# Half of the token stage's weights and its first two tiles loaded one stage earlier, and the order of that stage's opening

## The reference, cut to what matters

```
m = silu(cond) @ w_mod + b_mod                 # shift1, scale1, ...
h = rmsnorm(x, norm1_g) * (1 + scale1) + shift1
q, k, v, g = split(h @ w_in[:, 1536:3584], 4)  # 512 columns each
q, k = rope_2d(q), rope_2d(k * HD ** -0.5)
state = exp(log_sigmoid(decay) * 128) * state + (k * zeta).T @ v   # per tile of 128 tokens
```

## Time and profile before

| | |
|---|---|
| median of 3 runs | 3487.83 us (3487.07 to 3490.82) |
| the profiled execution's own time | 3487.38 us |
| its span | 3485.6 us |
| PE busy | 3204.7 us, 92% |
| DVE, ACT, POOL busy | 1608.5, 1276.7, 369.1 us |
| mean granted clock of PE | 0.954 of full speed |
| token stage | from 127 us to about 620 us of the span |

### The profile page before, as it was taken

How to read it: one execution, slowest core, us unless ns; L and a number is a source line. 1 busy time by engine, 2 the same in 40 slices (tenths; PEclk the granted TensorE clock), 3 DMA queues, 4 the chain that set the end, 5 groups by cost and what they waited for, 6 DMA issues and landing times. The chain is left out here.

```text
span 3485.6 us, 51370 instructions
## 1 busy us (share of the span) xinstructions
PE 3204.7 (92%) x19287; PEld 2742.7 (79%) x19287; DVE 1608.5 (46%) x2989; ACT 1276.7 (37%) x1947; POOL 369.1 (11%) x313
## 2 busy tenths in 40 slices
PE   7589999799979789999988982999999999999996
PEld 2278888798835779989987872988998898889895
DVE  5333223433345542332225557565555555556555
ACT  4544443322234031222114430444444444344445
POOL 1011111000033200000000001011111111112112
PEclk9899999999989789999999985999999999999998
DMA  9533332411199852341206442455555555555557
GB/s 337 193 119 107 105 123 86 147 56 62 56 324 346 284 174 84 99 128 60 93 31 213 151 141 81 162 196 202 197 194 187 178 183 172 171 172 200 195 205 277
DMA packets 281637, 565.66 MB, mean 162 GB/s; under 512 B 22296, under 2 KB 161432, under 8 KB 277289
## 3 DMA queue, kind: packets, MB, share of 16 engines
q1 hardware_dynamic: 257023, 503.83, 41.5%
q0 software_dynamic: 15456, 54.88, 5.3%
q10 hardware_dynamic: 8976, 4.46, 0.4%
HBM read 434.44 MB, written 128.64 MB: 162 GB/s over the span
## 5 line engine op out<-in xcount | busy, mean ns | idle before, releaser
L71 PE MATMUL experts_bank<-experts_xT_high,experts_w_high_gu 128*128 128x272 f32 x2048 | 598.6, 292 | 5.5 <-DVE experts_w_low_gu L2896 5.5
L73 PE MATMUL experts_bank<-experts_xT_high,experts_w_low_gu 128*128 128x272 f32 x2048 | 591.3, 289 | 0.0
L72 PE MATMUL experts_bank<-experts_xT_low,experts_w_high_gu 128*128 128x272 f32 x2048 | 589.9, 288 | 0.0
L71 PEld LDWEIGHTS experts_bank<-experts_xT_high,experts_w_high_gu 128*128 128x128 f32 x2048 | 386.2, 189 | 18.4 <-issue 12.2
L72 PEld LDWEIGHTS experts_bank<-experts_xT_low,experts_w_high_gu 128*128 128x128 f32 x2048 | 386.8, 189 | 4.0
L73 PEld LDWEIGHTS experts_bank<-experts_xT_high,experts_w_low_gu 128*128 128x128 f32 x2048 | 386.7, 189 | 0.0
L2896 DVE TENSOR_TENSOR experts_w_low_gu<-experts_w_raw_gu,experts_w_high_gu 128x1024 fp32r<-128x1024 f32 x256 | 302.2, 1215 | 12.5 <-ACT experts_w_high_gu L2695 12.4
L2695 ACT ACTIVATE experts_w_high_gu<-experts_w_raw_gu 128x1024 fp32r<-128x1024 f32 x256 | 257.4, 1047 | 19.7 <-DMA experts_w_raw_gu<-in_w_stream 19.6
L71 PE MATMUL merge_pg<-merge_hT_high,merge_w_gates_high 128*128 128x436 f32 (+1 forms) x640 | 231.9, 362 | 13.4 <-DVE merge_hT_low L2015 13.3
L72 PE MATMUL merge_pg<-merge_hT_low,merge_w_gates_high 128*128 128x436 f32 (+1 forms) x640 | 231.3, 361 | 0.0
L73 PE MATMUL merge_pg<-merge_hT_high,merge_w_gates_low 128*128 128x436 f32 (+1 forms) x640 | 230.9, 361 | 0.0
(11 more groups left out here) (385 smaller groups left out, 6627.5 us busy)
## 6 DMA issues: line engine op xcount, KB each, us to landing
experts_w_raw_gu<-in_w_stream SPq DMA_DIRECT2D x256, 512.0 KB
experts_w_raw_d<-in_w_stream SPq DMA_DIRECT2D x128, 512.0 KB, 6.3
filters_wm<-in_w_mod SPq DMA_DIRECT2D x12, 2048.0 KB, 12.8
merge_hT<-scratch_hT SPq DMA_DIRECT2D x32, 436.0 KB, 7.2
scratch_h<-out_row SPq DMA_DIRECT2D x17, 520.0 KB, 2.8
tokens_x<-in_xs SPq DMA_DIRECT2D x17, 512.0 KB, 5.3
scratch_hT<-tokens_hT SPq DMA_DIRECT2D x17, 512.0 KB, 4.4
scratch_qkT<-tokens_qkT SPq DMA_DIRECT2D x17, 512.0 KB, 2.8
```

The source lines that it names most:

```text
L71: pe.matmul(out, lhs[0], rhs[0], start=start, stop=False)
L72: pe.matmul(out, lhs[0], rhs[1], start=False, stop=False)
L73: return pe.matmul(out, lhs[1], rhs[0], start=False, stop=stop)
```

## The change

Eight of the 16 weight pieces are loaded in the filter stage. A new area `w_early` of eight pieces, with `x_early` and `rope_early` behind it, lies at the same addresses as `wm`: pieces 0 to 3 in its first slot, 4 to 7 in its second, x and the rotary tables of two tiles in the third. SP issues them when PE has used each slot for the last time: at p = 7 after chunk 9, at p = 9 after chunk 10, at p = 11 after chunk 11. Their semaphores live through all stages. In the token stage `qkT`, `vs`, `vz`, `gs`, `kvb`, `state`, `kvf` and `qk` are put at the start of memory, over `w_early`; x and rope are the early areas themselves. So the first state can be loaded only after all 16 pieces are split, and ACT's back(0) and DVE's turn(0) stand behind the splits.

The other eight pieces are loaded into the eight places of `w_early`, each after the piece that it replaces is split. ACT and DVE start with the front of tile 0 between the first splits, take the norm of tile 1 after eight of them, the rest of the splits, and only then the decays. The first two tiles' code is written out ahead of the loops. PE's own order is as it was.

```diff
+                    if p in (7, 9):
+                        sp.wait_ge(PM.sem, PM.at(9 if p == 7 else 10, "parts"))
+                        for m in range(4 * (p == 9), 4 + 4 * (p == 9)):
+                            n, k = PIECES[m]
+                            sp.dma_start(s["w_early"][:, m].rearrange("p (a b) -> p a b", b=512), d["w_qkvg"][n, :, k:k + 2, :])\
+                              .then_inc(s["ld_w_early"][m], 16)
+                    if p == 11:
+                        sp.wait_ge(PM.sem, PM.at(11, "parts"))
+                        for h in range(2):
+                            sp.dma_start(s["x_early"][:, h, :], d["xs"][take(h, 1)]).then_inc(s["ld_x_early"][h], 16)
+                            sp.dma_start(s["rope_early"][:, h, :], d["rope"][take(h, 1)]).then_inc(s["ld_rope_early"][h], 16)
...
+EARLY = 8
+TILE_WORDS = 17 * 512
+PIECES = [(n, k) for n in range(4) for k in range(0, KT, 2)]
...
+        "ld_w_early": [sem(f"ld_w_early{m}") for m in range(EARLY)],
+        "ld_x_early": [sem(f"ld_x_early{h}") for h in range(2)],
+        "ld_rope_early": [sem(f"ld_rope_early{h}") for h in range(2)],
     }
+
+    base = nc.sbuf_base
+    s["w_early"] = nc.alloc_sbuf_tensor_at("w_early", [P, EARLY, 1024], F32, offset=base)
+    s["x_early"] = nc.alloc_sbuf_tensor_at("x_early", [P, 2, DM], F32, offset=base + 4 * TILE_WORDS)
+    s["rope_early"] = nc.alloc_sbuf_tensor_at("rope_early", [P, 2, 512], F32, offset=base + 4 * (TILE_WORDS + 2 * DM))
+    return s
...
+        qkT = sb("qkT", [P, 2, 2, 512])
+        vs = sb("vs", [P, 2, 512])
+        vz = sb("vz", [P, 2, 512])
+        gs = sb("gs", [P, 2, 512])
+        kvb = sb("kvb", [P, 2, 512])
+        state = sb("state", [P, 2, 512])
+        kvf = sb("kvf", [P, 512])
+        qk = sb("qk", [P, 2, 512])
+        sb("early", [P, 2 * DM + 1024])
+        x = s["x_early"]
+        rope = s["rope_early"][:].rearrange("p a (b c) -> p a b c", b=4)
...
-                sp.dma_start(state[:, 0, :], d["state_f"]).then_inc(ldc, 16)
...
-                load_x(0, 0)
-                load_x(1, 1)
-                load_rope(0, 0)
-                load_rope(1, 1)
-                for m, (n, k) in enumerate(PIECES):
-                    if m >= 3:
-                        sp.wait_ge(w_dve, m - 2)
-                    sp.dma_start(staged[m % 3].rearrange("p (a b) -> p a b", b=512), d["w_qkvg"][n, :, k:k + 2, :])\
-                      .then_inc(ldw[m % 3], 16)
-                sp.wait_ge(ldc, 64)
+                for m in range(EARLY, len(PIECES)):
+                    n, k = PIECES[m]
+                    sp.wait_ge(w_dve, m - EARLY + 1)
+                    sp.dma_start(early[:, m % EARLY].rearrange("p (a b) -> p a b", b=512), d["w_qkvg"][n, :, k:k + 2, :])\
+                      .then_inc(ldw[m % EARLY], 16)
+                sp.wait_ge(w_dve, len(PIECES))
+                sp.dma_start(state[:, 0, :], d["state_f"]).then_inc(lds, 16)
+                sp.wait_ge(ldc, 48)
+                sp.wait_ge(lds, 16)
...
-                log_decays_scalar(act, tmp, ca, cv)
-                act.wait_ge(cv, 9)
-                for n in range(2):
-                    act.activation(zeta[:, 4 * n:4 * n + 4], lg[:, 4 * n:4 * n + 4], ACT.Exp, scale=expo[:, n:n + 1])\
-                       .then_inc(cs, 1)
-                act.activation(dec[:], lg[:], ACT.Exp, scale=float(P)).then_inc(cs, 1)
-                act.wait_ge(cs, 4)
-
-                def front(t, h, cond, k):
+                act.wait_ge(cs, 1)
+
+                def decays():
+                    log_decays_scalar(act, tmp, ca, cv)
+                    act.wait_ge(cv, 9)
+                    for n in range(2):
+                        act.activation(zeta[:, 4 * n:4 * n + 4], lg[:, 4 * n:4 * n + 4], ACT.Exp, scale=expo[:, n:n + 1])\
+                           .then_inc(cs, 1)
+                    act.activation(dec[:], lg[:], ACT.Exp, scale=float(P)).then_inc(cs, 1)
+
+                def split(m):
+                    n, k = PIECES[m]
+                    act.wait_ge(ldw[m % EARLY], 16 * (m // EARLY + 1))
+                    act.activation(wh[:, n, k:k + 2].rearrange("p a b -> p (a b)"), early[:, m % EARLY], ACT.Copy)\
+                       .then_inc(w_act, 1)
+
+                def norm(t, h, k):
...
-                front(0, 0, 0, 0)
-                for m, (n, k) in enumerate(PIECES):
-                    act.wait_ge(ldw[m % 3], 16 * (m // 3 + 1))
-                    act.activation(wh[:, n, k:k + 2].rearrange("p a b -> p (a b)"), staged[m % 3], ACT.Copy)\
-                       .then_inc(w_act, 1)
-                with act.Fori(0, LOOP // 2, 1) as i:
+                norm(0, 0, 0)
+                split(0)
+                scale(0, 0)
+                split(1)
+                split(2)
+                turned(0, 0, 0)
+                for m in range(3, EARLY):
+                    split(m)
+                norm(1, 1, 0)
+                scale(1, 1)
+                for m in range(EARLY, len(PIECES)):
+                    split(m)
+                decays()
+                turned(1, 1, 0)
+                act.wait_ge(w_dve, len(PIECES))
+                back_1(0, 0, 0)
+                front(2, 0, 0, 1)
+                back_1(1, 1, 0)
+                with act.Fori(1, LOOP // 2, 1) as i:
...
-                v.wait_ge(ldc, 64)
-                log_decays_vector(v, lg, raw, tmp, ca, cv)
-                v.wait_ge(cs, 4)
-
-                def front(t, h, cond, k):
+
+                def split(m):
+                    n, k = PIECES[m]
+                    v.wait_ge(w_act, m + 1)
+                    flat = lambda a: a[:, n, k:k + 2].rearrange("p a b -> p (a b)")
+                    v.tensor_tensor(flat(wl), early[:, m % EARLY], flat(wh).bitcast(F32), ALU.subtract).then_inc(w_dve, 1)
...
+                    if isinstance(t, int) and t == 0:
+                        v.wait_ge(lds, 16)
...
                 norm(0, 0)
-                front(0, 0, 0, 0)
-                for m, (n, k) in enumerate(PIECES):
-                    v.wait_ge(w_act, m + 1)
-                    flat = lambda a: a[:, n, k:k + 2].rearrange("p a b -> p (a b)")
-                    v.tensor_tensor(flat(wl), staged[m % 3], flat(wh).bitcast(F32), ALU.subtract).then_inc(w_dve, 1)
-                with v.Fori(0, LOOP // 2, 1) as i:
+                split(0)
+                split(1)
+                turned(0, 0, 0)
+                split(2)
+                low(0, 0)
+                for m in range(3, EARLY):
+                    split(m)
+                norm(1, 1)
+                for m in range(EARLY, len(PIECES)):
+                    split(m)
+                v.wait_ge(ldc, 48)
+                log_decays_vector(v, lg, raw, tmp, ca, cv)
+                v.wait_ge(cs, 4)
+                back_1(0, 0, 0)
+                front(1, 1, 0)
+                back_2(0, 0, 0)
+                norm(2, 0)
+                back_1(1, 1, 0)
+                front(2, 0, 0)
+                back_2(1, 1, 0)
+                with v.Fori(1, LOOP // 2, 1) as i:
...
```

More of the change, by code:

```diff
@@ L865, in front @@
                                    ACT.Copy).then_inc(*AF.inc("high"))
+                def front(t, h, cond, k):
+                    norm(t, h, k)
+                    scale(t, h)
+                    turned(t, h, cond)
                 def back_1(t, h, k):
@@ L918, in front @@
                      .then_inc(*VF.inc("low"))
+                def front(t, h, cond):
+                    turned(t, h, cond)
+                    low(t, h)
                 def norm(t, h):
@@ L972, in _ @@
                         back_1(i * 2 + h, h, i)
[L973 removed]
+                        front(i * 2 + (h + 1), 1 - h, 0)
                         back_2(i * 2 + h, h, i)
```

31 lines of the change are left out of this document (11 added, 20 removed).

## The result

The changed kernel takes 3453.41 us, the median of 4 runs (3451.82 to 3455.72), against 3488.66 us for four runs of the kernel before (3487.07 to 3490.82). The ratio is 0.9902, with a 95% interval of 0.989 to 0.9915. The forecast was 3456.5 us, in a range of 3451 to 3466. The profiled execution took 3455.72 us with a span of 3453.8, so between the two profiled executions (3487.38 before) the gain is 31.66 us, where 31.2 were worked out; between the two medians it is 35.25 us.

The account below looks back on a forecast made before the run. Weight loads through three landing places were taken to bound the token stage's opening; q(1) 32.3 us earlier, less 1.1 for the clock, gives 31.2 off 3487.4, rounded to 3456.5 us, range 3451 to 3466.

Parts of the forecast that it names:

- Filter stage, cost 0: Filter stage: 5.77 MB of added loads fit into free DMA slices and cost 0; 14.4 us if all lay open.
- Rival B: Filter stage: early loads delay the spectra's stores and hold ACT, giving 3462.5 us, or 3471 fully exposed; chance 8%.
- the prediction's own signs of a cost: Filter stage's end: `eps` memset outside 127 to 128 us, or ACT's waits for spectra stores beyond 5 us.
- To q(0): Token stage opening: ACT starts at about 127.5, and q(0) at 139.9 against 155.47, 15.5 us earlier.
- The splits: Weight splitting on DVE: after xn(1), eight subtractions at 1.235 us each, the last ending at 157.2.
- Decays, turn(0), hT(1), v: After the splits: decays 3.86 us, turn(0) 4.2, DVE's hT(1) done at 166.7, v copied out by 168.4.
- The added wait: hT of tile 1 waits for hT(0)'s store, queued on SP behind the state's load; costs 0 to 2.1 us.
- POOL: Before the kv products: first `vz` takes 1.02 us, so the first kv product starts at 169.5, the second at 170.6.
- The clock: PE rests from 166.5 to 169.5; if its clock falls q(1) loses 2.2 us, half charged, 1.1.
- The bound: Token stage opening: bound moves from loads to DVE's queue; PE's own row alone would put q(1) at 168.3.

Follow-up runs that it names:

- early store: Changed kernel with SP issuing the store of hT(0) between the loads of pieces 10 and 11, ahead of the state's load; 3454.14 us.
- the spare products: Changed kernel plus unread identity products on PE, 20 ahead of tile 0's transposes and 24 behind them; 3463.25 us, one run.
- the kernels with no wait of note in PE's row: Changed kernel with hT(0) stored early and DVE's hT(1) before turn(0), plus v copied first (3452.00 us) or decays moved to the filter stage (3451.88 us).

## Why the prediction was right, point by point

The path was right: the loads are no longer waited for, DVE's queue and the row behind it through ACT and POOL set q(1), and each step is within 2.3 us of its place. That the sum held to a tenth of a microsecond at q(1), 31.2 predicted and 31.21 measured, is luck: the splits, POOL, the clock and a later start of the whole stage were off, and cancelled. All times after `eps`:

| step | predicted | measured |
|---|---|---|
| q(0) starts | 12.65 | 12.02 |
| last subtraction ends | 29.95 | 27.84 |
| decays end | 33.85 | 31.63 |
| turn(0) ends | 38.05 | 35.95 |
| DVE's hT(1) ends | 39.45 | 37.24 |
| v copied | 41.15 | 38.87 |
| first kv product | 42.25 | 40.67 |
| q(1) | 44.15, 45.25 with the clock | 43.89 |

*Filter stage, cost 0: right, with a later start that is not its doing.* The eight pieces take 8.0 us each to land beside other traffic, and ACT's waits for the spectra's stores grow by 1.2 us:

```profile
w_early<-in_w_qkvg SPq DMA_DIRECT2D x8, 512.0 KB, 8.0
```
```profile
ACT filters_spec L448 <- DMA scratch_kspec<-filters_spec: 6.6, 2, 3.4
```
```profile
ACT filters_spec L437 <- DMA scratch_kspec<-filters_spec: 5.4, 2, 2.9
```

The second row is of the kernel after, the third of the kernel before. The bytes went into the free slices of the earlier trace rows:

```profile
GB/s 235 408 359 235 303 396 371 346 427 284 260 297 396 427 359 325 362 396 417 408 424 331 300 390 411 411 291 402 210 339 410 422 450 359 0 303 433 93 244 152
```

The mean between 75 and 128 us rose from 218 to 335 GB/s. Rival B's place for a cost was right, its price was not paid: from the first spectra's store to `eps` it is 67.28 us before and 67.30 after. The 1.33 us later start was there already at that first store (59.97 before, 61.28 after), before any early load is issued. In the ten experiments that store lies between 59.23 and 62.44 us and `eps` between 127.06 and 129.75, and the distance between the two is the same with early loads and without. Two of the prediction's own signs of a cost did show, `eps` at 128.58 in place of 127 to 128 and 6.6 us of waits for the stores in place of 5; by this distance neither was one.

*To q(0): right, 0.6 early.* ACT started 0.09 us after the memset (0.25 was taken). The copy of piece 0, behind ACT's table load, put 0.55 us between the square and `xn` (3.61 us in place of 3.06), where 0.76 was taken, so `xn` was 0.35 early at 3.70:

```profile
128.67 1.06 ACT L877 ACTIVATE tokens_xn<-x_early 128x1024 f32<-128x1024 f32 x1 [3.82 <-DVE tokens_eps L952]
129.64 0.19 ACT L877 ACTIVATION_READ_ACCUMULATOR tokens_xn<-x_early 128x1 f32 x1
129.84 1.28 ACT L880 ACT_TABLE_LOAD   x1
...
132.28 1.13 ACT L884 ACTIVATE tokens_xn<-x_early,tokens_rstd 128x1024 f32<-128x1024 f32 x1
```

The other 0.3 us came from DVE's steps, which followed each other more closely than I had taken.

*The splits: mis-sized by 2.1 us, to the good.* I took 1.235 us a subtraction, a little over the mean of 1.224 of ten, most of which followed a wait. In a row they take 1.15 (9.18 / 8, and 5.76 / 5 in the fronts), because the 1.22 us of one overlap its neighbour's by 0.07. Over the twelve subtractions from the fourth to the last that is 1.0 us; 0.6 was there at q(0), and 0.5 is hand-overs that I had put too high.

*Decays, turn(0), hT(1), v: right.* 3.88 us where 3.86 were taken, 4.29 for 4.2, 1.37 for 1.4, and `vs` within 0.2 us of its distance from hT(1).

*The added wait: right at 0.* The state's load took 2.5 us to land, the value taken; I had put the cost of the wait between 0 and 2.1 us. SP's rows after, and ACT's:

```profile
156.44 0.33 SPq L776 DMA_DIRECT2D tokens_state<-in_state_f  x1
159.49 0.70 SPq L746 DMA_DIRECT2D scratch_hT<-tokens_hT  x1
```
```profile
163.72 1.50 ACT L891 ACTIVATE tokens_hT<-tokens_tp,shift,scale 128x128 f32<-128x128 f32 x4 [3.51 <-issue]
165.90 1.06 ACT L897 ACTIVATE tokens_h_high<-tokens_hT 128x1024 fp32r<-128x1024 f32 x1 [0.68 <-ACT tokens_hT L891]
166.87 0.58 ACT L909 ACTIVATE tokens_vs<-tokens_pv 128x512 f32<-128x512 f32 x1
```

ACT did stand 3.51 us until the store had landed, 4.2 us after its issue (4.4 were taken), but `h_high(1)` needs DVE's half as well, and that ended at 165.82. The early store left the kv products where they were. The Trainium skill, in "DMA: Bandwidth & Descriptors", section "Anatomy of one DMA", has a fixed time plus a time for the bytes, which gave an estimate of 2.6 us for the state's load; that section is written for transfers that GpSimd issues, and this one is issued by SP. This trace's 2.5 is close to it all the same.

*POOL: mis-sized by 0.7 us.* Two `vz` took 2.04 us before and 2.49 now, and with the hand-overs the first kv product came 1.80 us after `vs` in place of 1.1.

```profile
167.62 2.49 POOL L1070 TENSOR_TENSOR tokens_vz<-tokens_vs,tokens_zeta 128x512 f32<-128x512 f32 x2 [60.09 <-ACT tokens_vs L909]
```

*The clock: near in size, wrong in place.* I charged 1.1 us to the projection q(1), half of 2.2, for a clock that might fall. It did fall, in the kv products: they took 3.22 us from the first to q(1), 1.3 more than at the upper clock, and q(1) itself lost about 0.2, for the clock was back at 1.00 from 173 us on. The rest that preceded it was 1.93 us and not 3. The Trainium skill, in "TensorE: Matmul & The Clock Gate", section "The HAM clock gate", has PE's clock fall after idleness, and says that the moment of a change is not tied to the kernel's own start and varies from run to run. The traces agree that the length of the rest alone does not settle it: at these same products the clock stayed at 1.00 after rests of 2.42 and 2.74 us and fell after 1.93 and 3.49.

So up to `vs` the stage ran 2.3 us ahead of my sum; POOL gave back 0.7 and the clock in the kv products 1.3, which leaves 0.3; the later start of the stage, which is not the change's doing, took 1.33, where 1.1 had been set aside for the clock. The 1.1 stood in the sum for another reason, so this agreement is luck. The median of the runs lies 2.3 us below the profiled execution, which the forecast could not know: the profiled one was the slowest of four.

*The bound.* The prediction said that the bound goes from the loads to DVE's queue, and that PE's own row would put q(1) at 168.3, which is 41.05 after `eps`. Both were shown: the spare products moved PE's row forward and q(1) followed DVE's, and the kernels with no wait of note in PE's row have q(1) at 40.30 and 40.77 (0.6 of the distance to 41.05 is the earlier q(0)).

*What the prediction did not see* is how the gain is shared. It followed one path and never asked which part of the change carries it. By the runs the loads in the filter stage are worth 6.9 us with the new order (8.2 at a like clock) and nothing with the old one, and the eight places are worth 21.8.

## What to carry to other kernels

When loads feed a split through few places and each place is refilled only after its piece is used, count places against landing time divided by the pace of the split: three places at 4.6 us per load held a 1.15 us step to 2.2 us, and eight removed nearly all of it without any earlier load. A prefetch gains where the work that needs it stands first in its engine's queue; here it was worth nothing behind 6 us of small loads and the decays. Reorder and prefetch together, and test each alone. A bound that is one wait ahead of the next, as here with POOL, ACT and PE within 4 us, gives little back for any single further edit.

## What the runs showed of the hardware

- PE's clock fell after a rest of 1.93 us in one execution and not after 2.42 us in another with the same products on both sides, nor after 2.74 us in a third, so the length of a rest alone did not decide it. In the spare-products kernel it fell after 3.49 us.
- When the clock fell, it did so after PE had begun again: the microsecond in which it stood idle shows 1.00, the next, with PE busy 0.75 of it, 0.75, and the two behind it 0.50. In finer stretches it is 0.98 from 169.25 to 169.50 us, where PE starts again, and 0.50 from there.
- Elementwise steps of 128x1024 f32 in a row cost less than one alone: 1.15 us against 1.22 on DVE, 0.96 against 1.06 on ACT, where eight copies take 7.68 us.

```profile
146.16 7.68 ACT L870 ACTIVATE tokens_w_high<-w_early 128x1024 fp32r<-128x1024 f32 x8
```

- In a single slice of 1.3 us the DMA engines moved 450 GB/s, and 335 on average over 53 us, with loads and stores mixed.
- Two executions of code that is the same, the stages behind the token stage, differed by 6.6 us (2858.3 and 2864.9), which is more than most of the edits here were worth.
